# Borders of a two-layer block: residual add from PSUM, split mean sum, earlier root table, composed scales, three tiles of squares

## The chip, the cores and the metric

One core of a Trainium2 chip runs the whole program. The metric is device time in microseconds, the median of three runs.

## What is computed

Two layers of a hybrid block over x of 512 tokens by 1024 channels, and then a second block (an mLSTM branch and a Fourier branch, with RMS norms) on the same x. What the change touches is the frame around each layer and the norms between the blocks:

```python
def hybrid_layer(x, ...):
    ada = c_act @ w_ada + b_ada
    shift, scale, gate = jnp.split(ada, 3, axis=-1)
    u = x * (1.0 + scale[:, None, :]) + shift[:, None, :]
    proj = jnp.einsum("bsd,dp->bsp", u, w_in)
    ...
    a = jax.nn.silu(layer_norm(a, ln_a_g, ln_a_b))
    ...
    m = g_a * y_a + g_b * y_b + g_c * y_c
    out = jnp.einsum("bsd,de->bse", m, w_o)
    return layer_norm(DEEPNORM_ALPHA * x + gate[:, None, :] * out, ln_g, ln_b)

# second block, before each branch and at the end
h = rmsnorm(x, norm_g[i]) * (1.0 + sc[:, None, :]) + sh[:, None, :]
```

## The kernel before

x lies channels by tokens, as eight tiles of 128 channels by 512 tokens (index j or k). Every product of weights is done with three matmuls (high by high, high by low, low by high part), helper `product`, lines 1882 to 1884. Weights come in 306 blocks of eight 128x128 tiles in a ring of three: SP loads a block (L358), ScalarE copies its high part (`split_to`, L451), GpSimd subtracts to get the low part (L391), TensorE waits for `weights_lo`. SP's queue holds these loads and those of `w_ada` in one written order; a `w_ada` load (L369) waits for VectorE's `products` (L1152, L1156), which make the next layer's shift, scale and gate along the way.

Each engine has its program written out by hand, in order; engines wait for each other on counters (`P`, `A`, `Dn` give the count at which TensorE, ScalarE, VectorE have done a labelled step). The steps around the change:
- Output product `wo` (TensorE, `first_chunks` and the loop behind it): eight chunks of 24 matmuls, into banks 0 and 1 in turn; the first two are made together, in `first_chunks`. ScalarE copies a bank, times the gate, to `tmp` (L743); TensorE's chunk j waits for the copy of j-2. VectorE adds `ALPHA * x_old` (L1523, label `r`) and keeps a running sum (L1528, `r_sum`). `x_old` overlays the `b` tiles: ScalarE issues its eight loads (L753) behind the wait for `wo` 0 and for the last `yb` product, in layer 1 followed by eight loads of the context (L760); VectorE waits for all eight ahead of `r` 0.
- Mean and squares: TensorE sums `tmp[3]` over partitions (`sum_rows`, L1952), VectorE subtracts (`x_cent`, L1536), ScalarE squares into two tiles in turn (L774), TensorE sums each, ScalarE takes the root (L776), VectorE the reciprocal (L1539).
- Layer 1 begins: per tile `x_norm` (VectorE L1237), `layer_out` (ScalarE L480: times `ln_g`, plus `ln_b`), `u` (VectorE L1261), `uH` (ScalarE L488), `uL` (VectorE L1093), interleaved; then ScalarE issues eight stores of x to `x_park` (L528), and copies `q_lat` out of PSUM (L533).
- In layer 1 the context is normed on the side (`nc`), its scaling on VectorE between `r` 6 and `r` 7.
- Norms `n0` (after layer 1), `n1` and `nf` (the last): squares (L497), sums (L1965), root (L501), reciprocal (L1217), scaled tile (L1230), high part (L507), low part (L1224). For `n0`, `layer_out` and square alternate on ScalarE.
- The norm inside branch `a` has squares L703, root L706, and the gates' tanh (`merge_gate`) between them.

## Time and profile before

| | |
|---|---|
| median of 3 runs | 2504.02 us (2499.62 to 2504.71) |
| profiled execution | 2502.21 us, span 2500.4 us |
| granted TensorE clock, mean | 0.962 of full speed |
| TensorE busy | 2292.0 us (92%) |
| VectorE, ScalarE, GpSimd busy | 1453.5 (58%), 859.6 (34%), 1073.2 us (43%) |

The profile shows one execution. Its times count from the span's start; layer 0 ends and layer 1 begins near 655, layer 1 ends near 1280, `n1` is near 2135. The busy shares are means over stages with different limits; the timeline rows below show, in square brackets, how long an engine was idle ahead of a row and what ended the idle time.

### The profile page before, as it was taken

How to read it: one execution, taken by the hardware profiler on the slowest of the kernel's cores; microseconds unless marked ns; L12 is line 12 of the kernel's file. 1: busy time of each engine (PE TensorE's matmuls, PEld its weight loads, DVE VectorE, ACT ScalarE, POOL GpSimd, SP SyncE). 2: the span in 40 equal slices, each digit the busy share in tenths (PEclk: the TensorE clock that was granted, in tenths of full speed). 3: DMA queues.
4: the chain of work that ended last, by engine and by line, in shares of the span. 5: the costliest groups of instructions: out<-in, count | busy, mean ns of one | idle time of the engine just before them, and what ended most of it. 6: DMA issues, size and time to landing. Idle time of an engine off the chain costs nothing.

```text
span 2500.4 us, 30577 instructions
## 1 busy us (share of the span) xinstructions
PE 2292.0 (92%) x10728; PEld 1858.6 (74%) x10728; DVE 1453.5 (58%) x2336; ACT 859.6 (34%) x1394; POOL 1073.2 (43%) x1276
## 2 busy tenths in 40 slices
PE   6799899999789989999967989889999999899997
PEld 3587777888568777788746878777778778688875
DVE  5899976432479997632268383654666766433211
ACT  2332334222442233422244333333443443333211
POOL 1555426555246543555405343432344343334333
PEclk8999999999899989999988999999999999999999
DMA  7343324443223222333302222223243242122222
GB/s 290 122 151 113 107 85 147 148 155 121 95 85 127 76 96 73 118 122 109 127 26 91 87 81 88 74 95 104 71 141 117 77 142 86 53 75 69 76 68 68
DMA packets 93203, 259.80 MB, mean 104 GB/s; under 512 B 10128, under 2 KB 11536, under 8 KB 92944
## 3 DMA queue, kind: packets, MB, share of 16 engines
q1 hardware_dynamic: 71392, 210.23, 26.3%
q10 hardware_dynamic: 21680, 47.79, 5.3%
q8 instruction: 86, 1.41, 0.2%
q14 instruction: 45, 0.37, 0.0%
HBM read 237.01 MB, written 20.97 MB: 103 GB/s over the span
## 4 chain that ended last, share of the span: by engine, by line
PE 49%; DVE 16%; issue 15%; POOL 12%; ACT 3%; ACTq 1%; DMA 0%; POOLq 0%; DVEq 0%; SPq 0%
PE bank L1882 15%; PE bank L1883 15%; PE bank L1884 15%; POOL t L391 11%; DVE t L1581 4%; DVE t L1378 2%; DVE t L1097 1%; DVE t L1093 1%; DVE t L1156 1%; PE bank L1952 1%; PE bank L1965 1%; POOL t L401 1%; PE bank L2242 1%; DVE t L1578 1%; DVE t L1101 0%
## 5 line engine op out<-in xcount | busy, mean ns | idle before, releaser
L391 POOL TENSOR_TENSOR t<-t,t 128x256 fp32r<-128x256 f32 x1208 | 1016.9, 873 | 1233.9 <-ACT t L451 1233.8
L1882 PE MATMUL bank<-t,t 128*128 128x512 f32 (+1 forms) x3056 | 1190.9, 390 | 95.3 <-POOL t L391 25.0
L1883 PE MATMUL bank<-t,t 128*128 128x512 f32 (+1 forms) x3056 | 1161.4, 380 | 0.0
L1884 PE MATMUL bank<-t,t 128*128 128x512 f32 (+1 forms) x3056 | 1157.9, 379 | 0.0
L1882 PEld LDWEIGHTS bank<-t,t 128*128 128x128 f32 x3056 | 590.0, 193 | 229.7 <-DVE t L1093 23.0
L1883 PEld LDWEIGHTS bank<-t,t 128*128 128x128 f32 x3056 | 590.1, 193 | 107.3 <-issue 5.0
L1884 PEld LDWEIGHTS bank<-t,t 128*128 128x128 f32 x3056 | 588.1, 192 | 108.9
L451 ACT ACTIVATE t<-t 128x1024 fp32r<-128x1024 f32 x302 | 317.2, 1054 | 244.1 <-PE bank L1884 190.6
L1156 DVE SCALAR_TENSOR_TENSOR t<-t,t,t 128x512 f32<-128x512 f32 x168 | 163.6, 987 | 114.9 <-DMA t<-w_ada 94.1
L1378 DVE SCALAR_TENSOR_TENSOR t<-t,t,t 128x512 f32<-128x512 f32 x240 | 200.7, 836 | 6.7
L1097 DVE SCALAR_TENSOR_TENSOR t<-t,bank 128x512 f32<-128x512 f32 x112 | 76.7, 685 | 186.8 <-PE bank L1884 88.6
L1581 DVE SCALAR_TENSOR_TENSOR t<-t,t,t 128x512 f32<-128x512 f32 (+1 forms) x160 | 143.4, 896 | 5.7
L1093 DVE TENSOR_TENSOR t<-bank,t 128x256 fp32r<-128x256 f32 (+1 forms) x136 | 70.9, 559 | 121.6 <-ACT t L1031 65.1
L1093 DVE TENSOR_TENSOR t<-t,t 128x512 fp32r<-128x512 f32 (+2 forms) x52 | 48.0, 940 | 94.6 <-ACT t L808 84.4
L590 ACT ACTIVATE t<-bank,t 128x128 f32<-128x128 f32 (+3 forms) x64 | 33.8, 529 | 197.5 <-DVE t L1351 197.3
L427 POOL TENSOR_TENSOR t<-t,t 128x256 fp32r<-128x256 f32 x48 | 41.0, 881 | 140.5 <-ACT t L830 140.5
L692 ACT ACTIVATE t<-bank 128x512 f32<-128x512 f32 x48 | 28.6, 596 | 137.9 <-PE bank L1884 137.9
L1101 DVE SCALAR_TENSOR_TENSOR t<-t,t 128x512 fp32r<-128x512 f32 x64 | 55.8, 881 | 34.2 <-ACT t L735 11.7
L2242 PE MATMUL bank<-t,t 128*128 128x512 f32 x96 | 38.3, 420 | 25.8 <-DVE t L1093 14.8
L2070 PEld LDWEIGHTS bank<-t,t 128*128 128x128 f32 x320 | 46.4, 200 | 16.9 <-ACT t L600 13.5
L1952 PE MATMUL bank<-t,t 128*128 128x512 f32 x88 | 44.5, 639 | 15.4 <-DVE t L1528 11.3
L1867 DVE SCALAR_TENSOR_TENSOR t<-bank,t,t 128x512 f32<-128x512 f32 x8 | 6.0, 751 | 83.8 <-PE bank L1884 83.8
(232 smaller groups left out, 1747.2 us busy)
## 6 DMA issues: line engine op xcount, KB each, us to landing
t<-blocks SPq DMA_DIRECT2D x306, 512.0 KB, 3.6
t<-w_ada SPq DMA_DIRECT2D x144, 256.0 KB, 2.7
t<-w_ada SPq DMA_DIRECT2D x20, 512.0 KB, 11.6
xm_park<-t ACTq DMA_DIRECT2D x16, 384.0 KB, 2.3
s_park<-t ACTq DMA_DIRECT2D x16, 384.0 KB, 2.3
t<-xm_park ACTq DMA_DIRECT2D x16, 384.0 KB, 4.4
t<-s_park ACTq DMA_DIRECT2D x16, 384.0 KB, 5.1
xc_park<-t ACTq DMA_DIRECT2D x16, 256.0 KB, 2.0
```

Of the source, the lines that this page charges most:

```text
L391: low = pool.tensor_tensor(w_lo[slot][:, part], w_raw[slot][:, part], w_hi[slot][:, part].bitcast(F32), ALU.subtract)
L451: act.activation(w_hi[b % RING][:], w_raw[b % RING][:], ACT.Copy).then_inc(weights_hi, 1)
L1093: dve.tensor_tensor(dst, src, hi.bitcast(F32), ALU.subtract).then_inc(dve_done, d(*label))
L1097: dve.scalar_tensor_tensor(dst, tanh, 1.0, by, ALU.add, ALU.mult).then_inc(dve_done, d(*label))
L1156: dve.scalar_tensor_tensor(acc[:], src[:], c, acc[:], ALU.mult, ALU.add).then_inc(ada_sums, 1)
L1378: dve.scalar_tensor_tensor(a_acc[:, j, :], src, V("conv_a_w", l, j * TAPS_A + k), a_acc[:, j, :], ALU.mult, ALU.add).then_inc(dve_done, d( ...
L1581: dve.scalar_tensor_tensor(out, src, w(k), out, ALU.mult, ALU.add).then_inc(dve_done, d())
L1882: pe.matmul(out, wh, xh, start=start, stop=False)
L1883: pe.matmul(out, wh, xl, start=False, stop=False)
L1884: return pe.matmul(out, wl, xh, start=False, stop=stop)
L1952: pe.matmul(bank[:], ones[:], tile, start=(j == 0), stop=(j == n - 1)).then_inc(pe_done, p(*label))
L2242: pe.matmul(banks[7][:], w, lat[n], start=(first and n == 0), stop=(last and n == 1))
```

## The change

- `wo`: ScalarE's copy is gone. VectorE computes `r` from the bank, times the gate, plus `x_old`; the gate is divided by ALPHA beforehand (`gate_over_alpha`) and the eps of the layer's norm by ALPHA squared (`eps_x`), so that `x_old` needs no factor. TensorE's chunk j waits for `r` j-2.
- The sum for the mean is made in two parts: the running sum of tiles 0 to 6, and tile 7 by itself.
- A one-column root (`root_ahead`) is put ahead of the squares, in branch `a`, at the end of layer 0, in `n1` and in `nf`. In branch `a` the root is also put ahead of `merge_gate(0, 0)`.
- Squares go into three tiles in turn (`sq_t`), at the ends of the layers and in `n0` and `n1`.
- Layer 1's `u` is made from the centred x in one step, with the norm's scale and bias composed with those of the layer (`input_scales`); its high and low parts add the bias. `x_norm` (now times `ln_g`) and `layer_out` (now only plus `ln_b`) come behind all eight low parts, and the stores to `x_park` behind them.
- `n0` squares x plus `ln_b` straight from `x_norm`; the eight `layer_out` come behind the root, four ahead of the high parts and four among them.

```diff
+            def root_ahead():
+
+                act.activation(spare[:], eps_rms[:], ACT.Sqrt).then_inc(act_done, a())
+
             def layer_out(l, j):
 
                 act.wait_ge(dve_done, Dn(l, "x_norm", j))
-                act.activation(x[:, j, :], x[:, j, :], ACT.Identity, bias=V("ln_b", l, j), scale=V("ln_g", l, j))\
-                    .then_inc(act_done, a(l, "y", j))
+                act.activation(x[:, j, :], x[:, j, :], ACT.Identity, bias=V("ln_b", l, j)).then_inc(act_done, a(l, "y", j))
 
             def u_high(l, j):
                 act.wait_ge(dve_done, Dn(l, "u", j))
                 if l and j == 0:
 
                     act.wait_ge(pe_done, P("block", B_Y(l - 1) + 35))
-                act.activation(uH[:, j, :], tmp[U_TMP[j % 3]][:], ACT.Copy).then_inc(act_done, a(l, "uH", j))
+                if l:
+                    act.activation(uH[:, j, :], tmp[U_TMP[j % 3]][:], ACT.Identity, bias=scale1[:, 1, j:j + 1]).then_inc(act_done, a(l, "uH", j))
+                else:
+                    act.activation(uH[:, j, :], tmp[U_TMP[j % 3]][:], ACT.Copy).then_inc(act_done, a(l, "uH", j))
...
-                    if l:
-                        layer_out(l - 1, j)
-                        if j:
-                            u_high(l, j - 1)
-                    else:
-                        if j == KT // 2:
-                            row_out(1)
-                        u_high(l, j)
+                    if l == 0 and j == KT // 2:
+                        row_out(1)
+                    u_high(l, j)
                 if l == 0:
                     act.wait_ge(dve_done, Dn("rope_angle"))
                     act.activation(rope[64:128, :], tmp[4][64:128, :], ACT.Sin).then_inc(act_done, a("rope_sin"))
                 if l:
-                    u_high(l, KT - 1)
+                    for j in range(KT):
+                        layer_out(l - 1, j)
...
+                root_ahead()
                 for j in range(NA):
                     act.wait_ge(dve_done, Dn(l, "a_cent", j))
                     if j >= 2:
...
                     else:
                         act.wait_ge(dve_done, Dn(l, "cL", NA - 1))
                     act.activation(tmp[j % 2][:], a_acc[:, j, :], ACT.Square).then_inc(act_done, a(l, "a_sq", j))
-                merge_gate(0, 0)
                 act.wait_ge(pe_done, P(l, "a_sq", NA - 1))
                 act.activation(tmp[2][:], banks[3][:], ACT.Sqrt, bias=eps_ln[:], scale=1.0 / WA).then_inc(act_done, a(l, "a_std"))
+                merge_gate(0, 0)
...
                     act.wait_ge(pe_done, P(l, "wo", j))
-                    if j >= 2:
-                        act.wait_ge(dve_done, Dn(l, "r", j - 2))
-                    else:
-                        act.wait_ge(dve_done, Dn(l, "aL", NA - 1))
-                    act.activation(tmp[j % 2][:], banks[j % 2][:], ACT.Copy, scale=ada[:, l, 2 * KT + j:2 * KT + j + 1])\
-                        .then_inc(act_done, a(l, "wo", j))
                     split_to(B_O(l) + j + 1 + RING)
                     if j == 0:
...
+                if l < L1 - 1:
+                    root_ahead()
                 for j in range(KT):
                     act.wait_ge(dve_done, Dn(l, "x_cent", j))
-                    if j >= 2:
-                        act.wait_ge(pe_done, P(l, "x_sq", j - 2))
-                    act.activation(tmp[j % 2][:], x[:, j, :], ACT.Square).then_inc(act_done, a(l, "x_sq", j))
+                    if j >= 3:
+                        act.wait_ge(pe_done, P(l, "x_sq", j - 3))
+                    act.activation(sq_t[j % 3][:], x[:, j, :], ACT.Square).then_inc(act_done, a(l, "x_sq", j))
                 act.wait_ge(pe_done, P(l, "x_sq", KT - 1))
-                act.activation(tmp[2][:], banks[3][:], ACT.Sqrt, bias=eps_ln[:], scale=1.0 / D).then_inc(act_done, a(l, "x_std"))
-
-            for j in range(KT + 1):
-                if j < KT:
-                    layer_out(L1 - 1, j)
-                if j:
-                    norm_squares(x, [j - 1], S, ("n0",), ready=lambda j: (act_done, A(L1 - 1, "y", j)))
+                act.activation(tmp[2][:], banks[3][:], ACT.Sqrt, bias=eps_x[:], scale=1.0 / D).then_inc(act_done, a(l, "x_std"))
+
+            for j in range(KT):
+                act.wait_ge(dve_done, Dn(L1 - 1, "x_norm", j))
+                if j >= 3:
+                    act.wait_ge(pe_done, P("n0", "sq", j - 3))
+                act.activation(sq_t[j % 3][:], x[:, j, :], ACT.Square, bias=V("ln_b", L1 - 1, j)).then_inc(act_done, a("n0", "sq", j))
             norm_std(S, KT, ("n0",), bank=5)
+            for j in range(KT // 2):
+                layer_out(L1 - 1, j)
             for j in range(KT):
                 norm_high(uH, j, S, ada[:, 2, j:j + 1], ("n0",))
+                if j + KT // 2 < KT:
+                    layer_out(L1 - 1, j + KT // 2)
...
+            root_ahead()
+            norm_squares(x, range(KT), S, ("n1",), sq_t, ready=lambda j: (dve_done, Dn("x2", MH - 1, j)))
...
+            root_ahead()
             norm_squares(x, range(KT), S, ("nf",), (f_s[0], f_s[1], f_rstd), ready=lambda j: (dve_done, Dn("x3", j)))
...
             def x_norm(l, j):
-                dve.tensor_tensor(x[:, j, :], x[:, j, :], tmp[2][:], ALU.mult).then_inc(dve_done, d(l, "x_norm", j))
+                dve.scalar_tensor_tensor(x[:, j, :], x[:, j, :], V("ln_g", l, j), tmp[2][:], ALU.mult, ALU.mult).then_inc(dve_done, d(l, "x_norm", j))
+
+            def gate_over_alpha(l):
+
+                gate = ada[:, l, 2 * KT:3 * KT]
+                wd()
+                dve.tensor_scalar(gate, gate, 1.0 / ALPHA, None, ALU.mult).then_inc(dve_done, d())
+
+            def input_scales(l):
+
+                wd()
+                dve.tensor_scalar(scale1[:, 1, :], ada[:, l, KT:2 * KT], 1.0, None, ALU.add).then_inc(dve_done, d())
+                wd()
+                dve.tensor_tensor(scale1[:, 0, :], scale1[:, 1, :], V("ln_g", l - 1, 0, KT), ALU.mult).then_inc(dve_done, d())
+                wd()
+                dve.tensor_tensor(scale1[:, 1, :], scale1[:, 1, :], V("ln_b", l - 1, 0, KT), ALU.mult).then_inc(dve_done, d())
+                wd()
+                dve.tensor_tensor(scale1[:, 1, :], scale1[:, 1, :], ada[:, l, 0:KT], ALU.add).then_inc(dve_done, d(l, "input_scales"))
...
+                for j in range(KT + 1 if l else 0):
+                    if j < KT:
+                        if j >= 3:
+                            wd(l, "uL", j - 3)
+                        dve.scalar_tensor_tensor(tmp[U_TMP[j % 3]][:], x[:, j, :], scale1[:, 0, j:j + 1], tmp[2][:], ALU.mult, ALU.mult)\
+                            .then_inc(dve_done, d(l, "u", j))
+                    if j:
+                        wa(l, "uH", j - 1)
+                        dve.scalar_tensor_tensor(uL[:, j - 1, :], tmp[U_TMP[(j - 1) % 3]][:], scale1[:, 1, j - 1:j], uH[:, j - 1, :].bitcast(F32),
+                                                 ALU.add, ALU.subtract).then_inc(dve_done, d(l, "uL", j - 1))
+                for j in range(KT if l else 0):
+                    x_norm(l - 1, j)
+
...
+                if l + 1 < L1:
+                    gate_over_alpha(l + 1)
+                    input_scales(l + 1)
 
                 dve.wait_ge(x_back, 16 * KT * (l + 1))
                 for j in range(KT):
-                    wa(l, "wo", j)
-                    dve.scalar_tensor_tensor(x[:, j, :], x_old[:, j, :], ALPHA, tmp[j % 2][:], ALU.mult, ALU.add)\
+                    wp(l, "wo", j)
+                    dve.scalar_tensor_tensor(x[:, j, :], banks[j % 2][:], ada[:, l, 2 * KT + j:2 * KT + j + 1], x_old[:, j, :], ALU.mult, ALU.add)\
                         .then_inc(dve_done, d(l, "r", j))
-                    if j:
+                    if 0 < j < KT - 1:
 
                         wd()
                         dve.tensor_tensor(tmp[3][:], x[:, 0, :] if j == 1 else tmp[3][:], x[:, j, :], ALU.add).then_inc(dve_done, d(l, "r_sum", j))
...
                 for j in range(2, KT):
-                    pe.wait_ge(act_done, A(l, "wo", j - 2))
+                    pe.wait_ge(dve_done, Dn(l, "r", j - 2))
                     chunk(banks[j % 2][:], [(B_O(l) + j, k, mH[:, k, :], mL[:, k, :]) for k in range(KT)], (l, "wo", j), (B_O(l) + j,))
                     if l == L1 - 1 and 3 <= j <= 5:
 
                         norm_sums(range(3 * j - 9, min(3 * j - 6, KT)), CTX, ("nc",), ctx_tmp, 4)
-                pe.wait_ge(dve_done, Dn(l, "r_sum", KT - 1))
-                sum_rows(banks[6], tmp[3][:], 1, 0, (l, "x_mean"))
+                pe.wait_ge(dve_done, Dn(l, "r_sum", KT - 2))
+                sum_rows(banks[6], tmp[3][:], 2, 0, (l, "x_mean_first"))
+                pe.wait_ge(dve_done, Dn(l, "r", KT - 1))
+                sum_rows(banks[6], x[:, KT - 1, :], 2, 1, (l, "x_mean"))
                 if l == L1 - 1:
 
                     context_tile(0)
                 for j in range(KT):
                     pe.wait_ge(act_done, A(l, "x_sq", j))
-                    sum_rows(banks[3], tmp[j % 2][:], KT, j, (l, "x_sq", j))
+                    sum_rows(banks[3], sq_t[j % 3][:], KT, j, (l, "x_sq", j))
```

## Rows read from the trace of the kernel before

**Rows 1.** The page: busy time of each engine, and a group of the costliest (line, count, mean ns).
```profile
PE 2292.0 (92%) x10728; PEld 1858.6 (74%) x10728; DVE 1453.5 (58%) x2336; ACT 859.6 (34%) x1394; POOL 1073.2 (43%) x1276
...
L1867 DVE SCALAR_TENSOR_TENSOR t<-bank,t,t 128x512 f32<-128x512 f32 x8 | 6.0, 751 | 83.8 <-PE bank L1884 83.8
```

**Rows 2.** Timeline, output product of layer 0 (start us, us, engine, line, [idle before <-releaser]).
```profile
605.99 0.50 PE L1882 MATMUL bank<-t,t 128*128 128x512 f32 x1
...
609.16 0.69 ACT L743 ACTIVATE t<-bank,t 128x512 f32<-128x512 f32 x1 [2.28 <-issue]
...
613.67 1.29 DVE L1523 SCALAR_TENSOR_TENSOR t<-t,t 128x512 f32<-128x512 f32 x2 [13.98 <-DMA t<-x]
```

**Rows 3.** Timeline, output product of layer 1.
```profile
1222.45 1.29 DVE L1523 SCALAR_TENSOR_TENSOR t<-t,t 128x512 f32<-128x512 f32 x2 [14.02 <-DMA t<-x_park]
...
1222.88 0.50 PE L1882 MATMUL bank<-t,t 128*128 128x512 f32 x1 [2.41 <-ACT t L743]
...
1230.07 1.02 PE L1965 MATMUL bank<-t,t 128*128 128x256 f32 x4
```

**Rows 4.** Timeline, end of layer 0: residual, mean, sums of squares, root.
```profile
639.69 0.69 DVE L1523 SCALAR_TENSOR_TENSOR t<-t,t 128x512 f32<-128x512 f32 x1 [4.02 <-ACT t L743]
...
641.16 1.13 PE L1952 MATMUL bank<-t,t 128*128 128x512 f32 x2 [2.23 <-DVE t L1528]
...
643.73 6.23 PE L1952 MATMUL bank<-t,t 128*128 128x512 f32 x10 [1.44 <-ACT t L774]
...
653.33 0.69 ACT L776 ACTIVATE t<-bank,t 128x512 f32<-128x512 f32 x1
```

**Rows 5.** Timeline, start of layer 1.
```profile
661.58 0.79 PE L1882 MATMUL bank<-t,t 128*128 128x512 f32 x1 [8.38 <-DVE t L1093]
...
670.32 5.21 ACTq L528 DMA_DIRECT2D x_park<-t  x8
...
679.51 0.60 ACT L533 ACTIVATE t<-bank 128x512 f32<-128x512 f32 x1 [8.56 <-PE bank L1884]
...
684.06 0.55 PE L1882 MATMUL bank<-t,t 128*128 128x512 f32 x1 [3.23 <-POOL t L391]
```

**Rows 6.** Timeline, from layer 1 to the second block.
```profile
1265.29 2.08 PE L1952 MATMUL bank<-t,t 128*128 128x512 f32 x2 [9.03 <-DVE t L1528]
...
1286.53 9.33 PE L1965 MATMUL bank<-t,t 128*128 128x512 f32 x16 [3.12 <-ACT t L497]
...
1295.90 0.69 ACT L501 ACTIVATE t<-bank,t 128x512 f32<-128x512 f32 x1 [1.40 <-PE bank L1965]
...
1302.35 0.79 PE L1882 MATMUL bank<-t,t 128*128 128x512 f32 x1 [6.49 <-DVE t L1224]
...
1310.25 1.63 DVE L1224 SCALAR_TENSOR_TENSOR t<-t,t,t 128x512 fp32r<-128x512 f32 x2
```

**Rows 7.** Busy time by windows, TensorE's granted clock first after the engines (then DMA share, GB/s).
```profile
661.58:667.30 5.72, 5.72 (x14) 4.48 (x15) 5.72 (x11) 4.42 (x8) 0.00 (x0) 0.51 0.00 0
667.30:680.80 13.50, 13.50 (x60) 10.86 (x58) 7.80 (x14) 4.44 (x7) 0.00 (x0) 1.00 0.73 253
```

**Rows 8.** Timeline of layer 0, mean and root of branch `a`, first product with `aL`.
```profile
384.88 3.59 PE L1952 MATMUL bank<-t,t 128*128 128x512 f32 x8
387.91 0.79 PE L1882 MATMUL bank<-t,t 128*128 128x512 f32 x1
...
397.82 1.28 ACT L706 ACT_TABLE_LOAD   x1
399.11 0.69 ACT L706 ACTIVATE t<-bank,t 128x512 f32<-128x512 f32 x1
...
425.97 0.50 PE L1882 MATMUL bank<-t,t 128*128 128x512 f32 x1 [1.18 <-DVE t L1101]
```

**Rows 9.** Timeline, sums of norm `n1`, and the last scalings of the kernel.
```profile
2129.81 7.70 PE L1965 MATMUL bank<-t,t 128*128 128x512 f32 x16 [1.75 <-ACT t L497]
...
2492.34 5.39 DVE L1874 SCALAR_TENSOR_TENSOR t<-t,t,t 128x512 f32<-128x512 f32 x8
```

More of the change, by code:

```diff
@@ L494, in norm_squares @@
                         act.wait_ge(*ready(j))
-                    if j >= 2:
-                        act.wait_ge(pe_done, P(*label, "sq", j - 2))
-                    act.activation(tmp[j % 2][:, 0:cols], tiles[:, j, :], ACT.Square).then_inc(act_done, a(*label, "sq", j))
+                    n = 3 if tmp is sq_t else 2
+                    if j >= n:
+                        act.wait_ge(pe_done, P(*label, "sq", j - n))
+                    act.activation(tmp[j % n][:, 0:cols], tiles[:, j, :], ACT.Square).then_inc(act_done, a(*label, "sq", j))
             def norm_std(cols, n, label, tmp=tmp, bank=3):
@@ L1218, in norm_recip, with norm_parts @@
                 wd()
-            def norm_parts(tiles, hi, lo, js, cols, shift, label, tmp=tmp):
+            def norm_parts(tiles, hi, lo, js, cols, shift, label, tmp=tmp, ready=None):
                 def low_part(j):
@@ L1229, in norm_parts @@
                         wd(*label, "uL", j - 2)
+                    if ready:
+                        wa(*ready(j))
                     dve.scalar_tensor_tensor(tmp[3 + j % 2][:, 0:cols], tiles[:, j, :], scale1[:, 1, j:j + 1], tmp[2][:, 0:cols],
@@ L1236, in x_norm @@
             def x_norm(l, j):
-                dve.tensor_tensor(x[:, j, :], x[:, j, :], tmp[2][:], ALU.mult).then_inc(dve_done, d(l, "x_norm", j))
-            for l in range(L1):
-                if l:
-                    wd()
-                    dve.tensor_scalar(scale1[:, 0, :], ada[:, l, KT:2 * KT], 1.0, None, ALU.add).then_inc(dve_done, d())
-                    wd()
-                for j in range(KT + 2):
-                    if l == 0 and j == KT // 2:
+                dve.scalar_tensor_tensor(x[:, j, :], x[:, j, :], V("ln_g", l, j), tmp[2][:], ALU.mult, ALU.mult).then_inc(dve_done, d(l, "x_norm", j))
[12 more added lines that the diff above has]
+                dve.tensor_tensor(scale1[:, 1, :], scale1[:, 1, :], ada[:, l, 0:KT], ALU.add).then_inc(dve_done, d(l, "input_scales"))
+            for l in range(L1):
+                for j in range(KT + 2 if l == 0 else 0):
+                    if j == KT // 2:
                         for i in (j - 2, j - 1):
@@ L1252, in _ @@
                         first_half(1)
[L1253 to L1262 removed]
+                    if j < KT:
+                        if j >= 3:
+                            wd(l, "uL", j - 3)
+                        dve.tensor_scalar(tmp[U_TMP[j % 3]][:], x[:, j, :], scale1[:, 0, j:j + 1], ada[:, l, j:j + 1],
+                                          ALU.mult, ALU.add).then_inc(dve_done, d(l, "u", j))
                     if j >= 2 and (l or j - 2 not in (KT // 2 - 2, KT // 2 - 1)):
@@ L1291, in _ @@
                     ada_out(0, 0, 2 * KT, KT)
+                    gate_over_alpha(0)
                     cd.also("first_gate")
@@ L1546, in _ @@
             norm_recip(S, ("n0",))
[L1547 removed]
+            norm_parts(x, uH, uL, range(KT), S, lambda j: ada[:, 2, j:j + 1], ("n0",), ready=lambda j: (L1 - 1, "y", j))
             wd()
@@ L1964, in norm_sums @@
                     pe.wait_ge(act_done, A(*label, "sq", j))
-                    pe.matmul(banks[bank][:, 0:cols], ones[:], tmp[j % 2][:, 0:cols], start=(j == 0), stop=(j == KT - 1))\
+                    tile = sq_t[j % 3] if tmp is sq_t else tmp[j % 2]
+                    pe.matmul(banks[bank][:, 0:cols], ones[:], tile[:, 0:cols], start=(j == 0), stop=(j == KT - 1))\
                         .then_inc(pe_done, p(*label, "sq", j))
@@ L2290, in _ @@
             context_tile(1)
-            norm_sums(range(KT), S, ("n0",), bank=5)
+            norm_sums(range(KT), S, ("n0",), sq_t, 5)
             for k in range(KT):
```

24 lines of the change are left out of this document (8 added, 16 removed).

## The prediction

> **What bounds the kernel now.** The first part of the page says that TensorE is busy for 92% of the span [rows 1]: time is mostly won or lost where TensorE stands still, or runs at half clock. So I listed TensorE's waits and read the timelines around each edited place, to see in each stretch which engine ended TensorE's wait. Five stretches are touched.
>
> At the output product (`wo`) of each layer TensorE hardly waits. In layer 0 its third chunk starts at 605.99, while VectorE's first residual add starts only at 613.67, held by the reload of `x_old` [rows 2]. ScalarE's copy out of PSUM decouples the two. In layer 1 the first residual add starts at 1222.45, and TensorE waits once in four chunks, 2.41 us at 1222.88, for the second copy, which ScalarE makes late because it first issues 16 DMAs [rows 3].
>
> At the layer borders the serial chain residual, mean, squares, root, scaling sets the time; TensorE idles or does only the small sums [rows 4 to 6].
>
> **The output product: a wait that replaces a copy.** The change removes the copy; VectorE reads the bank itself (`r`), and TensorE's chunk j waits for `r` j-2, for j from 2. `r` 0 stands behind the wait for all eight `x_old` tiles. Nothing starts these loads sooner: they overlay the `b` tiles, so they still wait for the last `yb` product, and in ScalarE's program they still stand behind the first `wo` product. Before, two finished banks were copied away while the loads were in flight; now TensorE must stand still.
> - Layer 0: `r` 0 starts at 613.67, takes 0.75 as a three-operand add from a bank does [rows 1], and 0.06 is the hand-over: TensorE goes on at 614.48 instead of 605.99 [rows 2]. That is +8.5. After such a stop its clock is low: behind the idle time of 8.38 before 661.58 the granted clock was 0.51, the 1.2 GHz level, for 5.7 us, and 14 matmuls took 5.72 where the next 60 took 13.50, 0.225 each [rows 5, 7]: 5.72 - 14 x 0.225 = 2.6 lost. Of the restarts that I read this is nearly the longest; I take 2.2. Sum +10.7.
> - Layer 1: restart at 1222.45 + 0.81 = 1223.26. Then two chunks of 24 matmuls, 10.8, and 2.2 of low clock: the third and fourth chunk end at 1236.3. Before they ended at 1230.07 [rows 3], after the wait of 2.41 and a low clock that the restart at 1222.88 already paid (7.19 for a chunk of 5.4). Net +6.2.
> Chunks behind these wait for an `r` that is long done, 5.4 us against 1.5. Both stops are lost in full, since no weight is awaited there. Bounds of the two together: 15.0 with no loss of clock beyond what is paid now, 18.
>
> **Border of the layers (0 to 1).** Of the chain mean, squares, root:
> - The mean. Before: copy (0.69), `r`, sum, then TensorE at 641.16 [rows 4]. After: `r` 7 straight from the bank as `wo` 7 ends, and only its own sum follows; the other seven tiles are summed during `r` 7. The copy and the `r_sum` fall away: -1.4.
> - The sums of squares. From the first one (643.73) to the root (653.33) are 9.60 [rows 4], 8 sums of two matmuls. With two tiles a square waits for the sum two before it. Unhindered, 8 such matmuls took 387.91 - 384.88 = 3.03, so 0.76 per sum [rows 8]; with three tiles 8 x 0.76 + 0.4 to deliver the last = 6.5. That is -3.1, or -2.1 if the first sum is at low clock as now; I take -2.9. So the root is 4.3 earlier.
> - The table load lay beside the last sum and is moved into ScalarE's wait before `x_cent` 0: nothing on the path.
> - Root to first product: 661.58 - 653.33 = 8.25 now [rows 4, 5]. The new form (scaled tile, high part, low part, no affine step between) is that of the norm ahead of the second block: 1302.35 - 1295.90 = 6.45 [rows 6]. -1.8.
> - Given back: `x_norm`, `layer_out` and the eight `x_park` stores now come behind all low parts. In the norm just named the last low part ends at 1311.88, 16.0 after its root [rows 6]; then 8 scalings of two tensors, 5.4 [rows 9], the last affine 0.8, and ScalarE issues DMAs for 5.2 (670.32) [rows 5]. It is blocked meanwhile, as it was until 609.16 [rows 2]. Its first copy of `q_lat`, and the weight splits queued behind it, come at root + 27.5. Now the copy comes at 679.51, root + 26.2 [rows 4, 5], and TensorE restarts at 684.06 on the low parts that GpSimd makes from these splits. So of 4.3 + 1.8 only 4.3 - 1.3 = 3.0 arrive. SP's w_ada and weight loads also wait for VectorE's products, now behind `x_norm`: about 3 later against the root, no later on the clock; they are covered unless the stores crowd them.
> Net -3.0; bounds -1 (clock low, loads late) and -5 (first sums fast, stores issued quickly).
>
> **Border to the second block (`n0`).** `r` 7 stands behind the context norm on VectorE, which starts one copy (0.7) sooner; the `r_sum` (0.7) goes: TensorE's 1265.29 becomes 1263.9 [rows 6], -1.4. The sums of `x_sq` stand behind a context product as before and gain 8 x 0.2 = -1.5. Then `n0`: now ScalarE makes an affine and a square per tile and feeds TensorE's sums, 1286.53 to the root at 1295.90 = 9.37 [rows 6]. After, the square reads x with its bias: the first starts 1.4 sooner, two affines of 0.7 standing ahead of it now, and the sums need 6.5 instead of 9.4, since VectorE (0.67 per scaling [rows 9]), ScalarE (about 0.6 per square) and TensorE (0.76) overlap. -4.3. The affines lie in the reciprocal (four of 0.7 in 3.35) and between the high parts (0.73 + 0.7 against VectorE's 1.45 per tile): at nothing, +0.5 at worst. Sum -7.2; bounds -5.5 and -8.
>
> **`a_std`, both layers.** Now the table load (1.28 at 397.82) and a tanh stand between the sums and the root [rows 8]; after, the load is under VectorE's `a_cent`, and the root is about 1.7 sooner. ScalarE's tanh of the affine is fixed by `mg` (0, 1), so of that 1.3 passes on; TensorE's wait for `aL` is 1.18 (425.97) [rows 8]. -1.2 per layer, -2.4; bounds 0 and -2.7. The later split behind `mg` (0, 0) is for a block that TensorE wants some 8 us later.
>
> **`n1` and the last norm.** In `n1` ScalarE comes from a weight split straight to the squares, so the load and the small root (1.5 together) now delay the first square, while the third tile shortens the sums, 7.70 for 16 matmuls [rows 9], by 1.5: +0.1, up to +2 if TensorE's longer pause there lowers its clock. The last norm keeps two tiles; its load goes ahead of a wait: +0.1, at worst +1.5. I take +0.5 together.
>
> **A rule against a row.** The Trainium skill, "ScalarE: Activation LUTs", section "What ACT_TABLE_LOAD costs", gives a switch of set 1.28 us and a drain of 1.38 besides. The trace shows the load, 1.28 at 397.82, and the root at 399.11 right behind it, no drain [rows 8]. By the page, an estimate, `a_std` would win up to another 1.4 per layer, of which TensorE's wait of 1.18 leaves nothing, and `n1` would lose 1.4 more: +6.2 in place of +4.8. I go by the row.
>
> **Small edits.** `gate_over_alpha` and `input_scales`, five tiny VectorE operations, lie in its idle 14 us before 613.67 [rows 2]; without that cover they would cost 1.5 per layer. The one of layer 0 lies in a wait for ScalarE.
>
> **Sum.** 10.7 + 6.2 - 3.0 - 7.2 - 2.4 + 0.5 = +4.8. The profiled execution took 2502.2 (span 2500.4, 1.8 around it), so 2507.0; it lies 1.8 below the median of 2504.02. I add the change to the median: **2508.8**.
>
> **Rivals.**
> 1. The stalls are as priced and the borders give their upper bounds (5 + 8 + 2.7): 16.9 - 15.7 + 0.5 = +1.7, 2505.7, no measurable difference; with the lower bound of the stalls, 15.0, -0.2 and 2503.8. For it: ScalarE may issue stores faster when SP's loads don't crowd them. Against: its blocked queue shows in the trace [rows 2, 5].
> 2. The borders give their lower bounds: 1 + 5.5, `a_std` hidden behind something else, and `n1` at low clock: 16.9 - 6.5 + 2 = +12.4, 2516.4. For it: the sums ran at low clock at the first border, and SP's loads queue behind the moved work. Against: three borders would have to go badly.
> 3. Other side: no stall at `wo`. If the eight loads had landed by 605.99, TensorE would not stop; then the sum is 4.8 - 16.9 = -12, 2492. It decides at loads 8 us earlier. Against it: the wait of 13.98 that VectorE has on them [rows 2], in both layers. The change doesn't move the loads ahead.
> 4. The stall is half made good later, by weights that are split and ready meanwhile: 4.8 - 8.5 = -3.7, 2500.3. Against: in layer 0 the chunks behind it run without waits now, so there is nothing to make good.
>
> **Chances.** Forecast (about +2.5 to +8) 0.55; rival 1 0.22; rival 2 0.12; rival 3 0.06; rival 4 0.05. 0.2%, 5.0 us, is about what a measurement of this kernel can tell from no change; my forecast stands just on that line. Slower by more: 0.32 of the forecast's 0.55, and rival 2, 0.44. Within: the other 0.23, 0.20 of rival 1 and 0.04 of rival 4, 0.47. Faster: rival 3 and the edges of 1 and 4, 0.09. Range 2500 to 2515; the forecast's own 2506 to 2512.
>
> **What the profile after would show.** TensorE idle about 8.5 us behind the second `wo` chunk in both layers, ended by VectorE's add, with a half clock behind it; sums of squares 0.76 apart; the first product of layer 1 some 6 us earlier against the end of `wo`, but the restart behind it only 3; `n0`'s root 7 earlier against the end of the context norm; no wait for `aL`. I am wrong if TensorE doesn't stop at `wo`, or if the border gains reach TensorE whole.

## The result and the profile after

The kernel after takes 2515.18 us, median of 7 runs (2507.23 to 2517.7), the kernel before beside it 2501.79 (2497.51 to 2504.71): ratio 1.0047, 95% interval 1.0032 to 1.0062 (the quotient of the two medians is 1.0054). It is slower by more than the 0.2% that a measurement can tell. Forecast were 2508.8 and a range that ends at 2515.

The profiled execution of after took 2515.23, its span 2513.4, 13.0 more than before's. To see where they come from I take the same event in both traces and read how far it has moved. The rows of after are given here in the order of the groups of before.

The page of after, first the busy times; they answer to [rows 1].
```profile
PE 2296.6 (91%) x10732; PEld 1866.8 (74%) x10732; DVE 1462.5 (58%) x2340; ACT 851.6 (34%) x1383; POOL 1070.1 (43%) x1276
```
No engine does much more or less. The 13 us are waits.

Timeline of after, output product of layer 0 (ACTq is ScalarE's DMA queue), against [rows 2].
```profile
604.39 3.72 ACTq L752 DMA_DIRECT2D t<-x  x8
...
614.23 1.41 DVE L1559 SCALAR_TENSOR_TENSOR t<-bank,t,t 128x512 f32<-128x512 f32 x2 [14.25 <-DMA t<-x]
...
615.03 0.80 PE L1918 MATMUL bank<-t,t 128*128 128x512 f32 x1 [10.11 <-DVE t L1559]
```
The same in layer 1, against [rows 3].
```profile
1232.73 1.41 DVE L1559 SCALAR_TENSOR_TENSOR t<-bank,t,t 128x512 f32<-128x512 f32 x2 [15.52 <-DMA t<-x_park]
...
1233.54 0.79 PE L1918 MATMUL bank<-t,t 128*128 128x512 f32 x1 [10.13 <-DVE t L1559]
...
1247.36 0.81 PE L2002 MATMUL bank<-t,t 128*128 128x256 f32 x3
```
Windows of after, the 7 us behind each pause and the 6.5 us that follow (granted clock first after the engines).
```profile
615.03:622.28 7.25, 7.25 (x25) 5.87 (x26) 1.30 (x2) 0.00 (x0) 0.00 (x0) 0.78 0.06 25
622.28:629.00 6.72, 6.72 (x32) 5.55 (x31) 2.65 (x4) 2.12 (x2) 2.94 (x5) 1.00 0.18 56
1233.54:1240.90 7.36, 7.36 (x20) 5.84 (x21) 1.87 (x2) 0.00 (x0) 2.49 (x3) 0.60 0.46 148
1240.90:1247.36 6.46, 6.46 (x31) 5.31 (x30) 1.44 (x2) 1.68 (x3) 2.93 (x4) 1.00 0.00 0
```
TensorE stands still for 10.1 us in both layers, until VectorE's first add, which waits for x. Then it computes at a mixture of its two levels, 1.2 and 2.4 GHz (0.78 and 0.60 of full speed). From the end of the first chunk to an event behind the pause (the end of chunk 7 in layer 0, the context sums behind chunk 3 in layer 1) takes 11.4 us more than before in layer 0, and 8.4 more in layer 1.

Timeline of after, end of layer 0 and start of layer 1, against [rows 4, 5].
```profile
649.32 2.13 PE L1988 MATMUL bank<-t,t 128*128 128x512 f32 x4
652.90 7.13 PE L1988 MATMUL bank<-t,t 128*128 128x512 f32 x16 [1.45 <-ACT t L775]
...
660.07 0.69 ACT L777 ACTIVATE t<-bank,t 128x512 f32<-128x512 f32 x1 [1.89 <-PE bank L1988]
...
666.61 0.80 PE L1918 MATMUL bank<-t,t 128*128 128x512 f32 x1 [6.57 <-DVE t L1301]
...
681.48 4.76 ACTq L532 DMA_DIRECT2D x_park<-t  x8
686.28 0.60 ACT L537 ACTIVATE t<-bank 128x512 f32<-128x512 f32 x1 [4.83 <-issue]
...
690.81 0.77 PE L1918 MATMUL bank<-t,t 128*128 128x512 f32 x1 [6.26 <-POOL t L392]
```
The mean no longer makes TensorE wait (before: 2.23 at 641.16 [rows 4]). From the first sum of squares to the root pass 7.17 us (before 9.60), from root to first product 6.54 (8.25). Then ScalarE issues stores for 4.8 us, and the copy at 686.28 comes at root + 26.21, as before (26.18, [rows 4, 5]). So the border gains 3.8 us: the shift against before falls from +10.55 at the end of the last chunk to +6.75 at TensorE's restart at 690.81.

Timeline of after, border to the second block and `n1`, against [rows 6, 9].
```profile
1281.07 2.08 PE L1988 MATMUL bank<-t,t 128*128 128x512 f32 x2 [6.66 <-DVE t L1559]
...
1300.53 8.83 PE L2002 MATMUL bank<-t,t 128*128 128x512 f32 x16 [1.87 <-ACT t L783]
...
1309.40 0.69 ACT L509 ACTIVATE t<-bank,t 128x512 f32<-128x512 f32 x1 [1.79 <-PE bank L2002]
1315.86 0.79 PE L1918 MATMUL bank<-t,t 128*128 128x512 f32 x1 [6.49 <-DVE t L1232]
...
2139.61 1.06 ACT L452 ACTIVATE t<-t 128x1024 fp32r<-128x1024 f32 x1 [4.38 <-PE bank L1920]
2140.69 1.28 ACT L480 ACT_TABLE_LOAD   x1
2141.98 0.20 ACT L480 ACTIVATE t<-t 128x1 f32<-128x1 f32 x1
...
2142.76 8.83 PE L2002 MATMUL bank<-t,t 128*128 128x512 f32 x16 [3.26 <-ACT t L505]
...
2151.62 0.69 ACT L509 ACTIVATE t<-bank,t 128x512 f32<-128x512 f32 x1 [1.89 <-PE bank L2002]
```
`n0`'s sums take 8.83 us with three tiles, hardly less than 9.33 with two. At `n1` TensorE's wait has grown from 1.75 to 3.26 and its sums from 7.70 to 8.83; the granted clock in their first 4.2 us is 0.65.
```profile
2142.76:2147.00 4.24, 4.24 (x7) 1.87 (x8) 0.00 (x0) 2.24 (x4) 0.76 (x2) 0.65 0.49 169
```

The `a` norm of layer 0, against [rows 8]; the root comes earlier (399.11 before), but TensorE's wait for `aL` is still there, 1.51 where it was 1.18.
```profile
396.40 0.69 ACT L710 ACTIVATE t<-bank,t 128x512 f32<-128x512 f32 x1 [1.22 <-PE bank L1988]
...
419.47 1.06 ACT L452 ACTIVATE t<-t 128x1024 fp32r<-128x1024 f32 x1 [5.60 <-DMA t<-blocks]
...
425.12 0.50 PE L1918 MATMUL bank<-t,t 128*128 128x512 f32 x1 [1.51 <-DVE t L1108]
```

### The profile page after: what moved, and what is told of

Same layout as the page of the kernel before. It is cut to its first block, busy times and chain, and to the rows that moved or that the text cites. A ratio compares the mean times of both kernels' runs of the same rounds, so it can differ in the third digit from the quotient of the medians.

```text
span 2513.4 us, 30559 instructions
## 1 busy us (share of the span) xinstructions
PE 2296.6 (91%) x10732; PEld 1866.8 (74%) x10732; DVE 1462.5 (58%) x2340; ACT 851.6 (34%) x1383; POOL 1070.1 (43%) x1276
## 4 chain that ended last, share of the span: by engine, by line
PE 52%; DVE 15%; issue 14%; POOL 11%; ACT 3%; DMA 0%; ACTq 0%; POOLq 0%; DVEq 0%; SPq 0%
PE bank L1918 16%; PE bank L1919 16%; PE bank L1920 15%; POOL t L392 11%; DVE t L1617 4%; DVE t L1411 1%; PE bank L2002 1%; DVE t L1104 1%; DVE t L1100 1%; DVE t L1164 1%; PE bank L1988 1%; PE bank L2281 1%; DVE t L1614 1%; PE bank L2098 0%; PE bank L2107 0%
## 5 line engine op out<-in xcount | busy, mean ns | idle before, releaser
L1100 DVE TENSOR_TENSOR t<-t,t 128x512 fp32r<-128x512 f32 (+2 forms) x44 | 42.6, 987 | 94.2 <-ACT t L813 85.6
L2281 PE MATMUL bank<-t,t 128*128 128x512 f32 x96 | 38.3, 420 | 25.8 <-DVE t L1100 14.7
L1559 DVE SCALAR_TENSOR_TENSOR t<-bank,t,t 128x512 f32<-128x512 f32 x16 | 11.8, 750 | 82.3 <-PE bank L1920 52.6
L2107 PE MATMUL bank<-t,t 128*128 128x64 f32 x320 | 46.7, 279 | 8.7 <-ACT t L604 8.7
## 6 DMA issues: line engine op xcount, KB each, us to landing
t<-w_ada SPq DMA_DIRECT2D x20, 512.0 KB, 11.6
```

Source lines behind the costliest of these rows:

```text
L1100: dve.tensor_tensor(dst, src, hi.bitcast(F32), ALU.subtract).then_inc(dve_done, d(*label))
L2107: mm = pe.matmul(banks[6 if u % 2 else 2][:, 0:VH], prob_t[:, u % 2, t * 128:(t + 1) * 128], v_tok[:, t, h * VH:(h + 1) * VH], start=(t == ...
L2281: pe.matmul(banks[7][:], w, lat[n], start=(first and n == 0), stop=(last and n == 1))
```

## Experiments

Two theories stood at the start. **A**: the add out of PSUM costs nearly 20 us, all at the two output products, and the other parts together are a gain. **B**: a good part of the loss is in the other parts. A third question came up on the way: what decides when TensorE runs at its lower level.

**Four banks.** After, with chunks in banks 0 to 3 in turn.
```diff
-                    pe.wait_ge(dve_done, Dn(l, "r", j - 2))
-                    chunk(banks[j % 2][:], ...)
+                    if j >= 4:
+                        pe.wait_ge(dve_done, Dn(l, "r", j - 4))
+                    chunk(banks[j % 4][:], ...)
```
and `r` reads `banks[j % 4]`.

> The kernel after, with the output chunks of each layer's last product going to four banks in turn, so that chunks 2 and 3 wait for no residual add and chunk j waits for add j-4. Theory A (TensorE stands still at the product after chunk 1 because bank 0 is free only once the first residual add, which waits for the reloaded x, has read it, and then computes two chunks at a lower clock): the pause of about 10.1 us in each layer goes, and the two slow chunks with it; by the landmarks of after (+11.4 and +8.4 us) the time comes to about 2495 us, 19 to 20 us below after and 6 to 7 below before. Rival B (the order of the landmarks misleads: the time goes to the load of x itself, which the adds of all chunks wait for, and VectorE then sets the end of the stage): the pause moves to chunk 4 and the border behind, and the time stays within 3 us of after. Rival C (the stall was only half of the loss, and the rest is a slower VectorE add that reads PSUM): 2503 to 2508.

**ScalarE's copy restored.** After, with the copy (gate as its scale) into two tiles, `r` reading them, TensorE waiting for copy j-2.

> The kernel after, with ScalarE's copy out of PSUM restored (gate as its scale, into two tiles) and TensorE waiting for the copy and not for the add; all else of the change stays. Theory A: the add out of PSUM costs 11.4 + 8.4 us, so this run lies 17 to 20 us below after, at 2495 to 2498, and 4 to 7 below before: the other parts together are a gain. Rival (the loss comes from the other parts, the roots loaded ahead and three tiles of squares, and the stall was made good behind): 2508 to 2515.

**The add out of PSUM alone.** Before, with `r` from the bank, the gate divided by ALPHA and TensorE waiting for `r` j-2; nothing else of the change.

> The kernel before, with only the residual add from PSUM (gate divided by alpha, add on VectorE straight from the bank, TensorE waits for the add). Theory A: +17 to +20 us against before, 2519 to 2522, with a pause of about 10 us at TensorE in each of the two layers and the next chunks at a lower clock. Rival (part of the loss is in the other edits): +8 to +13, 2510 to 2515.

**Work in the pause.** After, with this ahead of TensorE's wait for `r` 0.
```diff
+                    if j == 2:
+                        for i in range(10):
+                            pe.matmul(banks[4][:], ones[:], mH[:, 0, :].bitcast(F32), start=True, stop=True)
                     pe.wait_ge(dve_done, Dn(l, "r", j - 2))
```

> The kernel after, with ten products of ones (0.86 us each, about 8.6 us in all, into a bank that nothing reads) on TensorE ahead of its wait for the first residual add, in each layer: the pause stays as long but TensorE is busy in it. If the lower clock of the two chunks behind the pause (7.25 us for the first of them where others take about 5.2) comes from the pause, both chunks run at the full clock: 2 to 4 us in each layer, so 4 to 8 below after, at 2507 to 2511. If the clock falls there for another cause (or the ten products make the pause longer by as much as they give), the time is that of after within 2 us.

Measured, each against before in the same hour (an interval of 0.0013 to either side is some 3 us):

| kernel | median us | ratio to before, 95% interval |
|---|---|---|
| after | 2515.18 | 1.0047 (1.0032 to 1.0062) |
| four banks | 2493.92 | 0.9972 (0.9960 to 0.9984) |
| copy restored | 2495.03 | 0.9967 (0.9957 to 0.9977) |
| add out of PSUM alone | 2518.56 | 1.0064 (1.0051 to 1.0078) |
| work in the pause | 2506.54 | 1.0020 (1.0010 to 1.0031) |

The add costs 16.7 us alone (2518.56 - 2501.85), 0.4 below the range that I had written down, and taking it back, or giving it two more banks, is worth 20 to 21; by the intervals these sizes do not differ for sure. Theory A holds, B and the rival of a slower add fall: with four banks the add reads PSUM just the same, and both repaired kernels are faster than before. The lines below are TensorE's timeline in layer 0, first of the add alone, then of work in the pause.
```profile
616.37 0.80 PE L1882 MATMUL bank<-t,t 128*128 128x512 f32 x1 [10.11 <-DVE t L1523]
```
```profile
606.25 8.74 PE L2245 MATMUL bank<-t,t 128*128 128x512 f32 x20
616.24 0.50 PE L1918 MATMUL bank<-t,t 128*128 128x512 f32 x1 [1.24 <-DVE t L1559]
```
The pause stays as long, but the chunk behind it starts with matmuls of 0.50 and 0.40 and not 0.80 and 0.63, and the kernel gains 8.6 us on after (expected 4 to 8), though it does 17.5 us of useless work. By the events on both sides of the product (from the end of chunk 1 to the mean in layer 0, to the context sums in layer 1) it gains 1.6 and 3.15 us, 4.8 together, of which 0.45 is that the two pauses are 0.1 and 0.3 shorter. The other 3.8 come from places that the edit doesn't touch (`n0`'s sums, for one, take 7.13 in this trace and 8.83 in after). So of the 20 us between 4 and 5 were the lower clock, and the rest was the standing still.

With four banks TensorE goes through chunks 2 and 3 in layer 0 and has no wait before the mean; the restored copy does the same there, and in layer 1 leaves a wait of 3.65 us for the copy (2.41 before [rows 3]). With four banks, in layer 1 this row of its timeline shows a new wait, for the squares of the context norm.
```profile
1220.46 2.21 PE L2002 MATMUL bank<-t,t 128*128 128x256 f32 x6 [3.11 <-ACT t L505]
```

**Without the small roots.** After, with the four calls of `root_ahead()` removed.

> The kernel after without the four small roots that load the table ahead (a norm, layer 0's closing norm, n1 and the last norm); the order of the merge gates stays as in after. Theory A (at n1 ScalarE reaches the load right behind a weight split, so the load's 1.28 us and the root's 0.1 lie in front of the first square, TensorE waits 3.26 us where it waited 1.75, and its sums then run in part at the lower clock, 8.83 us for 16 matmuls): here the wait is 1.75 us again and the sums take at most 7.8; from the split to the big root of n1 passes 1 to 2.6 us less than in after (12.0 us), the root's own load of 1.28 included. At the last norm nothing changes (within 0.2 us), at layer 0's border and the a norm the root comes 1.3 us later. Rival (the slow sums at n1 are the clock's chance at that place): the sums take 8.8 us here too and n1 is 0 to 1.4 us longer than in after.

Time of the one run: 2507.94. Its timeline at `n1`:
```profile
2134.24 1.06 ACT L452 ACTIVATE t<-t 128x1024 fp32r<-128x1024 f32 x1 [4.38 <-PE bank L1915]
2135.20 1.65 ACT L505 ACTIVATE t<-t 128x512 f32<-128x512 f32 x3
2135.87 7.13 PE L1997 MATMUL bank<-t,t 128*128 128x512 f32 x16 [1.75 <-ACT t L505]
2141.17 1.28 ACT L509 ACT_TABLE_LOAD   x1
2143.04 0.69 ACT L509 ACTIVATE t<-bank,t 128x512 f32<-128x512 f32 x1 [0.59 <-PE bank L1997]
```
From the split to the root 8.80 us, in after 12.01 (from the split at 2139.61): the root loaded ahead costs 3.2 there, more than the 2.6 expected. And the expectation that the root comes 1.3 later at the other places is wrong: in layer 0 the load stands at 658.45, and the root starts at 660.32, still 7.17 behind the first sum, as in after. With three tiles ScalarE is done with its squares 1.9 us ahead of the root, and the load fits in there. At the last norm it makes no difference: from ScalarE's first activation to the root 8.52 us without the load ahead (2485.45 to 2493.97) and with it (2492.71, the small root, to 2501.23).

**Two tiles of squares.** After, with `sq_t = (tmp[0], tmp[1])`.

> The kernel after with two tiles of squares and not three, in the closing norms, n0 and n1. By the rows of after 16 matmuls of sums take 7.13 us with three tiles (0.43 each, TensorE the slower) and by those of before 7.6 to 7.7 with two: so 0.5 to 0.8 us more for each of the four norms where the clock is full, 2 to 3 in all, and nothing where the clock is low (8.8 either way). Rival (three tiles gain nothing, since ScalarE's square and its waits pace the sums anyway): 7.1 us with two tiles too.

TensorE's rows for the closing sums of layer 0 and for `n1`:
```profile
654.17 7.70 PE L1988 MATMUL bank<-t,t 128*128 128x512 f32 x16 [1.45 <-ACT t L775]
...
2138.36 9.21 PE L2002 MATMUL bank<-t,t 128*128 128x512 f32 x16 [3.26 <-ACT t L505]
```
7.70 against 7.13 and 9.21 against 8.83: the third tile gives 0.4 to 0.6 us per norm, at either clock (I had expected nothing at the low one). The one run took 2514.09; after's seven spread over 10 us, so the time says nothing.

**The mean in one piece.** After, with `if j:` for `if 0 < j < KT - 1:` and one product of ones.

> The kernel after with the mean as it was: VectorE adds the last chunk to the running sum, then one product of ones. From the end of chunk 7's matmuls to the first square of the closing norm, +1.4 us at layer 0 and at layer 1, by the add of 0.6 to 0.7 us and its two hand-overs (the step of the prediction). Rival (the second pair of matmuls and the add beside it hide each other): within 0.4 us.

Closing norm of layer 0, TensorE:
```profile
650.49 1.12 PE L1988 MATMUL bank<-t,t 128*128 128x512 f32 x2 [1.57 <-DVE t L1564]
653.06 9.90 PE L1988 MATMUL bank<-t,t 128*128 128x512 f32 x16 [1.45 <-ACT t L775]
669.53 0.79 PE L1918 MATMUL bank<-t,t 128*128 128x512 f32 x1 [6.57 <-DVE t L1301]
```
From the end of the last chunk (650.49 - 1.57) to the first sum: 4.14 us, in after 3.4 (649.48 to 652.90), before 4.80. So the split saves 0.7, where I had expected 1.4, and the copy that fell away another 0.65; in layer 1, from the end of the last chunk to the first sum, it saves 0.5. But the sums behind it take 9.90 and not 7.13: in all the split is worth 3.5 us at this place (20.6 against 17.1 from the last chunk to the first product). This is one trace; its run took 2521.39. The split doesn't do it by itself: with the copy restored and the mean split the same sums take 8.83. Before's sums, with neither, start at the lower level, as this window of before shows.
```profile
643.73:645.50 1.77, 1.77 (x2) 0.83 (x3) 1.77 (x4) 0.55 (x1) 0.01 (x1) 0.50 0.00 0
```

**What sets the lower clock.** The same 16 matmuls of sums, in the traces of all these kernels:

| place | TensorE's waits just before | sums, us | traces |
|---|---|---|---|
| closing norm, layer 0 | 1.45 | 7.13 | after and seven variants |
| same, two tiles | 1.45 | 7.70 | two tiles |
| same, two tiles | 1.57 and 1.45 | 10.28 | add alone |
| same, two tiles | 2.23 and 1.44 | 9.46, with a wait of 0.20 in it | before |
| same | 0.65 and 1.45 | 8.83 | copy restored |
| same | 1.57 and 1.45 | 9.90 | mean in one piece |
| `n1` | 1.75 | 7.13, two tiles 7.70 | all three without roots; before and add alone |
| `n1` | 3.26 | 8.83, two tiles 9.21 | after and five variants; two tiles |
| `n0` | 1.88 | 7.13 in five traces, 8.83 in five; two tiles 7.98 | |
| `n0`, old form, two tiles | 3.12 | 9.33; 10.11 | before; add alone |

Lines for three of these rows: the closing norm of the add alone; of before (the last six of its 16; the first ten are in [rows 4]); and `n0` with four banks.
```profile
654.98 10.28 PE L1952 MATMUL bank<-t,t 128*128 128x512 f32 x16 [1.45 <-ACT t L768]
```
```profile
650.16 3.03 PE L1952 MATMUL bank<-t,t 128*128 128x512 f32 x6 [0.20 <-ACT t L774]
```
```profile
1274.22 7.13 PE L2002 MATMUL bank<-t,t 128*128 128x512 f32 x16 [1.88 <-ACT t L783]
```
More standing still mostly goes with slower sums, but the length of the waits doesn't settle it: before waited longer than the add alone at the closing norm and had the faster sums, and at `n0` the same wait gives either. To test it where the pairing is cleanest, TensorE was given work at `n1`, ahead of the sums.
```diff
+            for i in range(3):
+                pe.matmul(banks[3][:], ones[:], uH[:, i, :].bitcast(F32), start=True, stop=True)
             norm_sums(range(KT), S, ("n1",), sq_t)
```

> The kernel after with three products of ones (0.86 us each, 2.6 in all, into the bank of the sums ahead of their first, whose start overwrites it) on TensorE where it waits 3.26 us for n1's first square. If the slow sums of n1 (8.83 us for 16 matmuls in all executions that wait 3.26 us there, 7.13 where the wait is 1.75) come from TensorE standing still, they take 7.1 to 7.3 us here, and n1's root comes 1.5 to 1.7 us earlier against the weight split than in after (10.4 instead of 12.0). Rival (the lower clock there has another cause): 8.8 us again, and 12.0.

TensorE's timeline there; the run took 2503.92.
```profile
2128.64 2.74 PE L2518 MATMUL bank<-t,t 128*128 128x512 f32 x6
2132.06 7.13 PE L2002 MATMUL bank<-t,t 128*128 128x512 f32 x16 [0.69 <-ACT t L505]
```
7.13, and the root 10.3 us behind the split, as expected (10.4): at `n1` it was the standing still. The single run's time says less: its pauses at the output products were 8.80 and 8.37 and not 10.1, for no reason that I know.

**Late stores.** Four banks, and layer 1's `x_park` stores issued behind the first key-value copy.

> The kernel with four banks, with layer 1's eight stores of x issued behind ScalarE's copy of the first key-value chunk and not ahead of the first query copy. Theory (ScalarE is held for 4.9 us by issuing them, the first query copy comes 4.9 us late and with it the weight splits and the next products): the first query copy comes about 4.4 us earlier, the product that waited 6.12 us for a weight part waits 2 to 4 us less, and the time is 2491 to 2492, 2 to 3 below the kernel with four banks (2493.9). Rival (the split behind it waits for the blocks to land anyway, a row shows 0.48 us of that wait): less than 1 us.

2492.42 us, ratio 0.9958 (0.9946 to 0.9971). ScalarE's timeline in it, with the first query copy:
```profile
670.98 0.60 ACT L534 ACTIVATE t<-bank 128x512 f32<-128x512 f32 x1 [2.37 <-PE bank L1921]
```
The copy now waits for TensorE and comes 17.2 us behind the first product, with four banks alone 19.7; I had expected 4.4 us earlier, and it is 2.5. TensorE's wait for GpSimd falls from 6.12 to 3.29. But 2.4 us there are 0.9 at the key-value sums, and in the time the 1.5 are inside what two medians differ by. A small gain at most.

**All three put together.** Four banks, late stores, no small roots.

> The kernel after with three edits: four banks at each layer's last product, layer 1's stores of x issued behind the first key-value copy, and none of the four small roots. The sum from the runs so far: 2492.4 us (four banks, late stores) less 3.2 us at n1, where the kernel without small roots went from the weight split to the root in 8.8 us and after in 12.0: 2489 to 2490, 12 to 13 us below before (ratio 0.995). Rival (the small roots' loads were a gain at the other three places, hidden by the clock): 2492 to 2494.

2492.82 us, ratio 0.9961 (0.9946 to 0.9976): not below the kernel with late stores, and inside the rival's 2492 to 2494. Its reason, loads ahead that were a gain at the other places, is not what the kernel without small roots showed. The gain at `n1` shows in the trace all the same: from the closing mean of layer 0 to the end 1850.8 us (span 2490.0, mean at 639.25), with late stores 1854.1 (2490.6, 636.49). The stretch ahead of that mean is nearly the same in all three kernels with four banks and took 634.8, 636.5 and 639.3 us: a spread of 4.5 that hides 3.4.

**TensorE kept busy.** The last kernel, and four times six products of ones where TensorE waits 6.5 us.
```diff
+            def warm(n, bank):
+                for i in range(n):
+                    pe.matmul(banks[bank][:], ones[:], vec[:, 0:512], start=True, stop=True)
...
             norm_sums(range(KT), S, ("n0",), sq_t, 5)
+            warm(6, 4)
```

> The kernel with four banks, late stores and no small roots, with six products of ones (0.86 us each, 5.2 in all, on a constant tile, into a bank that nothing reads) at four places where TensorE waits 6.5 to 6.7 us: for layer 1's last residual add, behind the closing sums of layer 0, behind n0's sums and behind n1's. Theory (TensorE falls to the lower clock after it stood still, and the first products behind such a wait take 0.43 us where later ones take 0.23): the products behind these waits run at the full clock from the first, about 2 us less at each place, 6 to 8 in all: 2485 to 2487, against 2492.8 without. Rival (the full clock comes back at another time only, or the added products push the ones behind them back): within 2 us of 2492.8.

2481.27 us, ratio 0.9915 (0.9900 to 0.9931), better than expected and the fastest of all. Windows of 4.7 to 5.1 us behind three of the four places (granted clock first after the engines), first without this work, then with it:
```profile
656.53:661.60 5.07, 5.07 (x14) 4.02 (x15) 5.07 (x8) 2.62 (x4) 0.00 (x0) 0.59 0.00 0
1293.45:1298.20 4.75, 4.75 (x11) 3.78 (x12) 4.64 (x7) 4.28 (x7) 0.00 (x0) 0.50 0.00 0
2133.34:2138.40 5.06, 5.06 (x12) 4.00 (x13) 4.96 (x8) 2.17 (x3) 0.00 (x0) 0.50 0.00 0
```
```profile
654.91:660.00 5.09, 5.08 (x22) 4.25 (x23) 5.09 (x8) 2.64 (x4) 0.00 (x0) 1.00 0.00 0
1288.29:1293.00 4.71, 4.71 (x20) 3.46 (x21) 4.60 (x7) 4.28 (x7) 0.00 (x0) 1.00 0.00 0
2124.93:2130.00 5.07, 5.07 (x21) 3.78 (x22) 4.96 (x8) 2.17 (x3) 0.00 (x0) 1.00 0.00 0
```
In the same time 20 to 22 matmuls instead of 11 to 14, at clock 1.00 and not 0.50 to 0.59. By the events behind them the four places give 2.5, 2.8, 2.1 and 1.9 us, 9.2 together; the two medians are 11.6 apart, the two profiled spans 9.0.

## Why the prediction was right in sign and wrong in size

The sum had the right sign and the right chief term. Its size was over 8 us short: +4.8 forecast, +13.4 between the two medians. That the time lies only 0.2 above the range is luck, for before's own median was 2501.79 this time and not the 2504.02 that I had added to; the range left room for +11. Of rival 2 (2516.4), to which I gave 0.12, two parts came, `a_std` without effect and `n1` at low clock. Its other part did not come as told: the first border gained more than forecast, the second less than my bound for the bad case, and the stalls cost 19.8, more than the 18 that I had as their upper bound. Term by term, in the profiled executions:

| term | predicted | in the trace of after |
|---|---|---|
| `wo`, layer 0 | +10.7 | +11.4 |
| `wo`, layer 1 | +6.2 | +8.4 |
| border 0 to 1 | -3.0 | -3.8 |
| border to `n0` | -7.2 | -2.7 |
| `a_std`, two layers | -2.4 | +0.5 |
| `n1` and last norm | +0.5 | +1.9 |
| sum | +4.8 | +15.7 |

The traces differ by 13.0; the rest, about -2.7, is drift in stretches that the change doesn't touch, 1.2 of it ahead of the first mean.

- **The output product.** "TensorE must stand still" is shown: 10.1 us in each layer, ended by `r` 0, and four banks or the copy take it away. The lower clock was put at 2.2 per layer, and the work in the pause gives 4.3 to 4.8 for both. What is missing is in good part x: in both layers the restart came 1.4 later behind the product than worked out from before's adds (in layer 1 VectorE's wait grew from 14.02 [rows 3] to 15.52). Why x landed later isn't known. In layer 1 the two chunks behind it took 13.8 where I had 13.0. (My lower bound of 15.0 for both layers doesn't follow from its rows either: 8.5 and, with the 1.8 of low clock paid before, 5.8 make 14.3.)
- **The sums of squares.** The step that failed is "8 such matmuls took 387.91 - 384.88 = 3.03, so 0.76 per sum". The row itself says 3.59 for the eight; the next product starts before they are done, and 3.03 is seven starts, 0.43 each. A sum takes 0.86, 16 matmuls 7.13, and two tiles take 7.70. So the third tile is worth 0.6 and not 1.5. What made 9.60 out of 7.7 in layer 0 before was the clock, and it took the split mean and the missing copy together to win that back (7.13 with both, 8.83 with the split alone, 9.90 with the missing copy alone). So it is luck that the sums at this border gave 2.4 of the 2.9 forecast: 0.6 is the third tile, the rest the clock, where my working gave it 1.0 at most.
- **Border to `n0`.** Of -7.2 the mean gave -1.5 as forecast (-1.4), the closing norm's sums of squares -0.5 (forecast -1.5), and `n0` -1.75 (forecast -4.3), because its sums ran at the lower clock. Another 1.1 was lost behind it. In the executions where those sums ran at the full clock (four banks, without roots) they take 7.13; so the term would be -1.5 - 0.5 - 3.45 = -5.5 at best, my own bound for the bad case.
- **Border 0 to 1.** The mean gave -1.4 as forecast, root to first product -1.7 (forecast -1.8). Then the moved work and the stores gave back 1.7, where I had put 3.1: the copy comes at root + 26.2 as before, and not at + 27.5, since the eight stores took 4.8 and the work ahead of them less than I had added up. That is why the border gave -3.8 and not -3.0. Late stores show that issuing them holds the copy (2.5 us of it back).
- **`a_std`.** The root came earlier, as forecast, and nothing followed: TensorE's wait for `aL` is 1.51. The step "1.3 passes on" took the chain behind the root to be bound by the root. With no root loaded ahead the same stretch (first mean to that product, 41.5 us) is as long as in after (41.4). What ends it wasn't tested; ScalarE waits 5.60 for a weight block at 419.47, as before (5.49 at 420.33), which speaks for the weights' arrival.
- **`n1`.** The delay of the first square (+1.5) and the low clock behind it are shown, both: 3.2 us, of which the third tile gives 0.4 to 0.6 back.
- **The rule against the row.** After shows the load at 2140.69 for 1.28 and the next activation at 2141.98, nothing between. The row was right to go by; the drain of 1.38 in the Trainium skill ("ScalarE: Activation LUTs", section "What ACT_TABLE_LOAD costs") shows in none of these rows, nor at 397.82 in [rows 8].

## What to carry to other kernels

Before a copy out of PSUM is taken away because another engine can read the bank itself, ask what that engine waits for: the copy was a buffer of two chunks between TensorE and a late transfer, and two more banks, where they are free, do the same. Where TensorE is the bound, a pause can cost more than its length: a change that saved 0.7 us of waiting was worth 3.5 at one place, in one trace, and work that nobody reads was worth 9 to 12 of 2493 us. And a load moved ahead of a wait is free only if the engine arrives there early: at `n1` it arrived just in time, and the load stood in the path.

## What the runs showed that I had not expected

- Small waits count. Waits of 1.57 and 1.45 us ahead of the sums gave 9.90 us for 16 matmuls (one trace), one of 1.45 alone gave 7.13 (eight).
- The same wait does not always give the same clock: at `n0`, behind 1.88 us, 8.83 in five traces and 7.13 in five. The Trainium skill ("TensorE: Matmul & The Clock Gate", section "What's actually happening") says that the number of slow matmuls at a kernel's start varies from run to run of the same kernel; these ten traces, of variants of one kernel and at a place far inside it, fit that but don't repeat it. What decides it at `n0` stays open.
- Useless matmuls in the pauses raised the mean granted clock from 0.962 to 0.970 and took 9 to 12 us off a kernel whose TensorE was already busy for 92% of the span.
- The stretch ahead of layer 0's closing mean varies by 4.5 us between executions of nearly the same instructions, so a gain of 3 us is better read between two events behind it than in the time.
